# Gating the output weights on GpSimd behind a raw sample mix, and reading the residual from PSUM by halves

## The reference

```python
mod = (c @ w_mod + b_mod)[:, None, :]
sh1, sc1, g1, sh2, sc2, g2 = jnp.split(mod, 6, axis=-1)     # one c for the prompt, another for the sample
...
pool_out, new_pool = _pool_mixer(u, hist_pool, past, w_pool, pool_scale)
attn = _stick_breaking(q, k_all, v_all, q_pos, k_pos).reshape(b, n, SB_WIDTH)
mix = jnp.concatenate([pool_out, attn], axis=-1) @ w_out    # (n, 1024) @ (1024, 1024)
x = _layer_norm(ALPHA * x + (1 + g1) * mix, ln1_g, ln1_b)
hn2 = (_norm(x) * (1 + sc2) + sh2).astype(x.dtype)
```

## Time and profile before

| | |
|---|---|
| median of 3 runs | 804.96 us (803.8 to 807.6) |
| the profiled execution | 804.16 us, its span 802.4 us |
| granted TensorE clock, mean | 0.979 |
| busy in the span | PE 767.7, DVE 562.9, ACT 374.6, POOL 309.9 us |
| block B | from 231 to about 490 us |
| first and last mix (M0 of tile 0, M1 of tile 8) | 299.1 us, 481.0 us |

### The profile page before, as it was taken

How to read it: one execution, slowest core, us unless ns; L and a number is a source line. 1 busy time by engine, 2 the same in 40 slices (tenths; PEclk the granted TensorE clock), 3 DMA queues, 4 the chain that set the end, 5 groups by cost and what they waited for, 6 DMA issues and landing times. The chain is left out here.

```text
span 802.4 us, 13449 instructions
## 1 busy us (share of the span) xinstructions
PE 767.7 (96%) x4808; PEld 606.4 (76%) x4809; DVE 562.9 (70%) x621; ACT 374.6 (47%) x706; POOL 309.9 (39%) x261
## 2 busy tenths in 40 slices
PE   7999999999989899999999997799999999999995
PEld 4889999999975566767767786488888888888641
DVE  5759957762125995876787867998656999574178
ACT  4571212212246983554464528544444444544254
POOL 2100799990010300100000110367565899564156
PEclk9999999999999999999999996899999999999997
DMA  8947644715049701320202249967779998889695
GB/s 320 388 153 257 210 158 133 228 53 185 1 149 327 236 2 53 106 80 27 80 27 79 80 158 333 338 249 262 259 269 361 415 376 270 294 315 364 238 372 200
DMA packets 78442, 168.59 MB, mean 210 GB/s; under 512 B 6974, under 2 KB 32126, under 8 KB 76219
## 3 DMA queue, kind: packets, MB, share of 16 engines
q1 hardware_dynamic: 69154, 134.36, 47.9%
q0 software_dynamic: 8048, 29.36, 9.9%
q10 hardware_dynamic: 1192, 4.21, 1.5%
HBM read 132.57 MB, written 33.12 MB: 207 GB/s over the span
## 5 line engine op out<-in xcount | busy, mean ns | idle before, releaser
L2501 PE MATMUL psum<-we_hi,x_parts 128*128 x384 | 136.5, 402 | 0.8 <-ACT x_parts L2257 0.8
L2045 DVE TENSOR_TENSOR we_lo<-we_raw,we_hi 128x2048 fp32r<-128x2048 f32 x48 | 118.0, 2461 | 1.5
L490 PE MATMUL psum<-hn_hi,w_hi 128*128 128x364 f32 (+1 forms) x380 | 91.2, 332 | 1.3 <-DVE hn_lo L716 1.3
L490 PE MATMUL psum<-hn_lo,w_hi 128*128 128x364 f32 (+1 forms) x380 | 90.3, 329 | 0.0
L490 PE MATMUL psum<-hn_hi,w_lo 128*128 128x364 f32 (+1 forms) x380 | 90.0, 328 | 0.0
L2044 DVE CAST we_hi<-we_raw 128x2048 fp32r<-128x2048 f32 x44 | 59.6, 1355 | 39.5 <-DMA we_raw<-in_w_up_dram 25.6
L1279 PE MATMUL psum<-wo_hi,mixin 128*128 128x512 f32 (+1 forms) x256 | 82.9, 395 | 1.6 <-DVE logits L1646 1.1
L2501 PEld LDWEIGHTS psum<-we_hi,x_parts 128*128 128x128 f32 x384 | 72.1, 188 | 15.3 <-issue 1.1
L2501 PE MATMUL psum<-we_lo,x_parts 128*128 x192 | 75.4, 393 | 0.0
L793 DVE SCALAR_TENSOR_TENSOR proj<-early,cT,proj 128x2048 f32<-128x2048 f32 x28 | 72.1, 2616 | 1.5 <-DMA early<-in_w_mod_dram 1.3
L490 PEld LDWEIGHTS psum<-hn_hi,w_hi 128*128 128x128 f32 x380 | 66.6, 189 | 4.7 <-issue 2.3
(11 more groups left out here) (376 smaller groups left out, 1569.2 us busy)
## 6 DMA issues: line engine op xcount, KB each, us to landing
we_raw<-in_w_up_dram SPq DMA_DIRECT2D x32, 1024.0 KB, 8.4
early<-in_w_mod_dram SPq DMA_DIRECT2D x16, 1024.0 KB, 5.4
we_raw<-in_w_down_dram SPq DMA_DIRECT2D x16, 1024.0 KB, 7.0
w_raw<-in_w_in_dram SPq DMA_DIRECT2D x16, 512.0 KB, 6.2
we_raw<-ff_d SPq DMA_DIRECT2D x12, 512.0 KB, 7.2
proj<-in_x_prompt_dram SPq DMA_DIRECT2D x4, 1024.0 KB, 8.0
sc_room<-in_w_mod_dram SPq DMA_DIRECT2D x4, 1024.0 KB, 11.0
wo_raw<-in_w_out_dram SPq DMA_DIRECT2D x2, 2048.0 KB, 9.4
```

What stands on the lines that cost most here:

```text
L490: mm = pe.matmul(psum[:, 2 * c + slot, 0:n], w[:, slot, k, :], hn[:, k, t0:t0 + n], start=(k == 0 and w is w_hi and hn is hn_hi), stop=(k ...
L2045: dve.tensor_tensor(we_lo[:, a:b], raw, we_hi[:, a:b].bitcast(F32), ALU.subtract).then_inc(ready, 1)
L2501: mm = pe.matmul(psum[:, bank, :], x[:, s, k, :], w[:, bass.ds(at + k * 2 * DE, 2 * DE)], start=(k == 0 and x is x_hi and w is we_hi), sto ...
```

## The change

The sample's mix no longer uses split weights. It becomes the step MS, in four parts at steps 10 to 13: float32 matmuls on `w_out` as loaded, with the two column halves in partitions 0 to 63 and 64 to 127 of bank 7. C0 and C1 of the sample follow at DVE steps 14 and 15, with the sample's gate now in the room of ln1_b. The 48 split matmuls of the sample, its Ph and its Pl are gone.

After the sample's mix GpSimd multiplies the prompt's gate into the eight chunks of `w_out` in place. The splits wh and wl wait for this and move from steps 13 to 22 and 15 to 25 to steps 16 to 23 and 17 to 24. For the prompt's tiles C0, C1 and R become R0 and R1: each reads a half of the mix from PSUM and adds ALPHA times x, with a row sum each; the two sums meet in the operation that makes the mean. The pieces PM are reordered (the sample's four first), GpSimd's constants come before the gates, and the mixes of tiles 1 to 7 move up (M0 of tile 1 from step 31 to 28).

```diff
 DVE_BESIDE = {
-    1: "DV:0", ... 14: "DV:8", 15: "wl:0", 16: "wl:1", 18: "wl:2", ... 25: "wl:7", 26: "Pl:0", 28: "C0:0",
+    1: "DV:0", ... 14: "DV:8 C0:0", 15: "C1:0", 17: "wl:0", 18: "wl:1", ... 24: "wl:7", 26: "Pl:1", 27: "R:0", 28: "E1:0 G1:0 R0:1",
...
+        g1s = l1b
...
+        PIECES = [(g, SEQ, DEC) for g in range(4)] + [(g, t0, 512) for g in range(4) for t0 in (0, 512)]
+        RAW_PARTS = 4
...
-            for dst, src in (mod_row(g1, 1, 2), (l1g, ...), mod_row(sc2, 1, 4), mod_row(sh2, 1, 3)):
+            for dst, src in (mod_row(g1, 0, 2), (l1g, ...), mod_row(sc2, 1, 4), mod_row(sh2, 1, 3)):
                 sp.dma_start(dst, src).then_inc(rows_in, 16)
             sp.wait_ge(pv_done, sample_units)
             sp.dma_start(*x_rows(0)).then_inc(xb_loaded, 16)
-            sp.dma_start(l1b, ln1_b[0].partition_broadcast(P)).then_inc(rows_in, 16)
+            for dst, src in (mod_row(g1s, 1, 2),):
+                sp.dma_start(dst, src).then_inc(g1_in, 16)
...
+            for n in range(KC):
+                k = WO_ORDER[n]
+                pool.wait_ge(rows_in, 16 * 4)
+                pool.wait_ge(mix_done, 2)
+                pool.tensor_tensor(wo_raw[:, k, :], wo_raw[:, k, :], g1, ALU.mult).then_inc(wo_gated, 1)
...
+            def mix_sample(m):
+                if m >= RAW_PARTS // 2:
+                    pe.wait_ge(att_copied, 2 * (m - RAW_PARTS // 2 + 1))
+                if m == 0:
+                    pe.wait_ge(pool_copied, 4)
+                    for half in range(2):
+                        pe.wait_ge(wo_loaded[half], 16)
+                    take("MS", 0, (mix_copied, 2))
+                for k in range(m * KC // RAW_PARTS, (m + 1) * KC // RAW_PARTS):
+                    for half in range(2):
+                        mm = pe.matmul(psum[DEC * half:DEC * half + DEC, 7, :], proj[:, k, SEQ:NT],
+                                       wo_raw[:, k, 512 * half:512 * half + 512], start=(k == 0), stop=(k == KC - 1))
+                if m == RAW_PARTS - 1:
+                    mm.then_inc(mix_done, 2)
...
             def high_wo(n):
-                act.wait_ge(wo_loaded[k // 4], 16)
+                act.wait_ge(wo_gated, n + 1)
...
-            def copy_mix(n, half):
+            def gate_sample(half):
+                dve.wait_ge(mix_done, 2)
+                dve.wait_ge(g1_in, 16)
+                at = slice(DEC * half, DEC * half + DEC)
+                gate = g1s[at, 512 * half:512 * half + 512]
+                dve.tensor_tensor(tile_of(0)[:, 4 * half:4 * half + 4, :], by_chunk(psum[at, 7, :]), by_chunk(gate),
                                   ALU.mult).then_inc(mix_copied, 1)
...
+            def residual(n, half):
+                r, part = rows(ORDER[n]), slice(4 * half, 4 * half + 4)
                 dve.wait_ge(xb_loaded, 16 * (n + 1))
+                dve.wait_ge(mix_done, 2 * n + half + 1)
+                total = (more_sums if half else sums[0])[0:r, n:n + 1]
+                dve.scalar_tensor_tensor(out=tile_of(n)[:, part, :], in0=by_chunk(xb)[0:r, part, :], scalar=ALPHA,
+                                         in1=by_chunk(bank(f"M{half}", n)[0:r, :]), op0=ALU.mult, op1=ALU.add,
+                                         accum_out=total).then_inc(mix_copied, 1)
```

More of the change, by code:

```diff
@@ L1093, in _ @@
                     sp.wait_ge(mix_copied, 2)
-                    for dst, src in (mod_row(g1, 0, 2),):
-                        sp.dma_start(dst, src).then_inc(g1_in, 16)
+                    sp.dma_start(l1b, ln1_b[0].partition_broadcast(P)).then_inc(rows_in, 16)
                 if n == TILES - 1:
@@ L1353, in _ @@
                         pool_map(n)
+                    elif step == "MS":
+                        mix_sample(n)
                     elif step in ("M0", "M1"):
@@ L1456, in square @@
                 if of == 0 and n + 1 < TILES:
-                    act.wait_ge(res_ready, n + 1)
+                    if n == 0:
+                        act.wait_ge(res_ready, 1)
+                    else:
+                        act.wait_ge(mix_copied, 2 * n + 2)
                     act.dma_start(*x_rows(n + 1)).then_inc(xb_loaded, 16)
@@ L1588, in centre @@
                 r = rows(ORDER[n])
-                dve.tensor_scalar(mean[of][0:r, n:n + 1], sums[of][0:r, n:n + 1], -1.0 / D, None, ALU.mult)
-                dve.tensor_scalar(mean32[of][0:r, n:n + 1], sums[of][0:r, n:n + 1], -1.0 / (32 * D), None, ALU.mult).then_inc(summed[of], 1)
-            def residual(n):
-                r, x = rows(ORDER[n]), tile_of(n)
-                dve.wait_ge(xb_loaded, 16 * (n + 1))
-                dve.wait_ge(mix_copied, 2 * n + 2)
-                dve.scalar_tensor_tensor(out=x, in0=by_chunk(xb)[0:r], scalar=ALPHA, in1=x, op0=ALU.mult, op1=ALU.add,
-                                         accum_out=sums[0][0:r, n:n + 1]).then_inc(res_ready, 1)
-                dve.wait_ge(res_ready, n + 1)
-                centre(0, n)
+                for dst, size in ((mean[of], D), (mean32[of], 32 * D)):
+                    if of == 0 and n:
+                        ins = dve.tensor_scalar(dst[0:r, n:n + 1], sums[of][0:r, n:n + 1], more_sums[0:r, n:n + 1], -1.0 / size,
+                                                ALU.add, ALU.mult)
+                    else:
+                        ins = dve.tensor_scalar(dst[0:r, n:n + 1], sums[of][0:r, n:n + 1], -1.0 / size, None, ALU.mult)
@@ new lines, in centre, with residual_sample @@
+                ins.then_inc(summed[of], 1)
+            def residual_sample():
+                r, x = DEC, tile_of(0)
+                dve.wait_ge(xb_loaded, 16)
+                dve.wait_ge(mix_copied, 2)
+                dve.scalar_tensor_tensor(out=x, in0=by_chunk(xb)[0:r], scalar=ALPHA, in1=x, op0=ALU.mult, op1=ALU.add,
+                                         accum_out=sums[0][0:r, 0:1]).then_inc(res_ready, 1)
+                dve.wait_ge(res_ready, 1)
+                centre(0, 0)
+            def residual(n, half):
+                r, part = rows(ORDER[n]), slice(4 * half, 4 * half + 4)
+                dve.wait_ge(xb_loaded, 16 * (n + 1))
+                dve.wait_ge(mix_done, 2 * n + half + 1)
[3 more added lines that the diff above has]
+                                         accum_out=total).then_inc(mix_copied, 1)
+                if half:
+                    dve.wait_ge(mix_copied, 2 * n + 2)
+                    centre(0, n)
@@ L1610, in scale_up @@
                     dst, row = scaled_of(n)[0:r], l1g
+                    if n == 0:
+                        dve.wait_ge(rows_in, 16 * 4)
                 else:
@@ L1663, in _ @@
                     elif step in ("C0", "C1"):
-                        copy_mix(n, int(step[1]))
+                        gate_sample(int(step[1]))
                     elif step == "R":
-                        residual(n)
+                        residual_sample()
+                    elif step in ("R0", "R1"):
+                        residual(n, int(step[1]))
                     elif step in ("E1", "E2"):
```

48 lines of the change are left out of this document (21 added, 27 removed), and 39 rows, old and new, of tables (ACT_BESIDE, DVE_BESIDE, PE_BESIDE).

## The result

| | before | after |
|---|---|---|
| median of 5 runs each, us | 805.84 (803.8 to 807.6) | 826.76 (825.65 to 827.03) |
| ratio of the two | | 1.0256, interval 1.0236 to 1.0276 |
| profiled execution: its time, span | 804.2, 802.4 | 827.0, 825.3 |
| value rows' transfer lands (DVE goes on) | 254.46 | 254.76 |
| first prompt mix starts | 317.08 (step 31) | 320.43 (step 28) |

What follows compares the result with a forecast made beforehand. DVE was taken to bound ahead of the first mix, PE from first to last mix. A 22 us delay less 12.5 saved (11.3 + 1.2) gave +9.5 on 804.2, 813.7, median 814 us; range 801 to 820.

Steps and rivals of the forecast that it cites:

- The delay D: First prompt mix against the sample's first mix at 299.1 us: starts at 321, 22 us later; above 12.5 means slower.
- the parts of MS: On PE ahead of the first mix: column halves overlap, about 1.9 us per part, four parts 7.5 us.
- the wait for bank 7: On PE in step 16: the first PM piece waits for C1 to free the bank, between 277 and 286 us.
- the end of the gates: On GpSimd: eight products of 2.37 us from about 267.5 us, stretched by turns with DVE, the last ending near 291.
- The gates in turns: Ahead of the first mix: GpSimd's gates and two-input DVE instructions exclude each other, adding 17.6 us; forecast case, chance 0.55.
- The scans are in: DVE's scans, with two SBUF inputs, also take turns with GpSimd's gates; held about three to one.
- a DVE list that ends at 302: DVE's list ahead of the first mix without gates: 267.4 plus 34.8 us of work, before adding 17.6.
- Nothing else of this size hides there: From first to last mix: PE is full, idle only 1.6 us, so all 11.3 us of sample mix come off.
- the mix doesn't lose what it should: Rival in the mixes: DVE or ACT become the bound there; dropped for DVE's 50 us to spare, no chance given.
- D of 9.5: Rival with gates in DVE's gaps, chance 0.17: PE alone decides, first mix at 308.5, 9.5 us later, net -3 us.
- The tail: Behind the last mix: one half residual of 0.8 us replaces product and residual, so 1.2 us comes off.

Runs made afterwards that it cites:

- 5: Kernel after without gates in the output weights, gate products from PSUM and full residuals as before, order lists of before from step 26 on: 807.54 us, ratio 0.9997 to before.
- 4: Kernel after with the order lists of the kernel before from step 26 on, all else as after: 819.48 us, ratio 1.0151 to before.
- 6: Kernel after without the eight gate products and with the order lists of before from step 26 on: 809.06 us, ratio 1.0014 to before.
- 1: Kernel after with the eight gate products on GpSimd left out: 816.57 us, ratio 1.0136 to before.
- kernel 7: Kernel after with each gate product on GpSimd replaced by memsets of about the same length: 817.74 us, ratio 1.0103 to before.
- 8: Kernel after with tile 5's second-norm square on ScalarE and the small DVE operation following it one step later: 821.22 us, ratio 1.0163 to before.
- 9: Raw sample mix alone in the order lists of before, its four parts at steps 8, 9, 10 and 12: 809.52 us, ratio 1.0022 to before.
- 11: Raw sample mix alone, parts early, lists of before; both sample gate products at DVE step 14, first PM piece behind them at step 17: 805.98 us, ratio 0.9988 to before.

## Why the prediction was wrong in size

The difference in E parts as follows, each step from a pair of kernels: the raw sample mix ahead of the mixes instead of M0 and M1 in them +2.4 us (5 against before), the gates' turns +9.4 (4 against 6), the re-timed lists +6.9 (after against 4): 18.7, measured 18.6. The steps form a chain from before to after, so they must add up; the check is that the other way round gives nearly the same, 8.8 us for the gates (after against 1) and 7.4 for the lists (1 against 6). Up to 2 us of the first step are the slow first part of kernels 5 and 6, and belong to the gates instead. With 0.3 us of later landing and a tail 4.0 us longer that is the span's 22.9, where the sum had 9.5: of the missing 13.4 us 8.2 stand ahead of the last mix's end, which came 18.9 us later where 22 less 11.3 had been forecast, and 5.2 behind it.

- **The delay D, right in number, in part by luck.** 21.3 us against 22. Within it the parts of MS (1.9 us forecast, 1.94 measured), the wait for bank 7 (283.4, forecast between 277 and 286) and the end of the gates (290.7, forecast 291) came as said; without gates D is 10.9 (kernel 1, corrected for the landing), forecast 9.5.
- **The gates in turns, right in kind.** The scans are in, which I had at three to one. Their size was too large: I counted 17.6 us exposed. DVE's busy time up to the first low part rose by 14.3 us (22.5 against 8.2 in kernel 7, which takes 269.62 to 281.34 with 3.25 and 0.46 us idle); kernel 7's idle 3.3 us lay under them, and 11.0 us came through to the first low part, 10.2 to the first mix. That the sum was right nonetheless is luck, two errors that cancel: I added 17.6 to a DVE list that ends at 302, which isn't where the first mix stands without gates: there PE's own list and its wait for bank 7 put it near 309.
- **"Nothing else of this size hides there": the step that failed.** I let all 11.3 us of the sample's mix come off behind the first mix. 2.4 came off. The prediction has PE full there, so that each microsecond of matmul taken out comes off the end. The rival "the mix doesn't lose what it should" was in the text and I dropped it, because DVE had 50 us to spare: an argument from a sum of busy time, against waits that are decided one at a time. The waits come from the lists, in which the prompt tiles' mixes and norms stand two to five steps earlier, beside other units' scans and copies (the square of tile 5 in step 48 instead of 53). There it stands in front of ACT's attention copy while DVE is not yet done with what it needs. With the lists of before PE idles for 1.5 us and 6.9 of the lost 8.9 us are back (experiments 4, 5, 6), with one square moved 3.2 of them (8). I had looked at these lists for what they do ahead of the first mix only.
- **The 11.3 us against MS's cost, too kind even so.** In the lists of before the exchange costs 2.4 us (5) where D of 9.5 less 11.3 had promised a gain of 1.8. Bank 7 and the clock that PE loses around it are most of it: with the parts early the cost is 1.9 (9), and with the bank freed a step earlier and asked for a step later the exchange gives 1.5 us of E (11).
- **The tail, wrong.** Of the 1.2 us promised behind the last mix 0.4 came: a logits addition now stands ready between the half residual and the scale-up and waits 0.44 us for PE, and the next step waits 0.33 for the square. The tail as a whole is 4.0 us longer: the stretch to the first experts 51.0 us against 48.6, the last stretch 48.3 against 46.7, with 226.0 us of experts equal between them. These are the stretches whose clock is not full (0.77 and 0.85, before 0.79 and 0.89):

```profile
499.99:551.00 51.01, 39.96 (x319) 30.47 (x319) 40.60 (x98) 30.80 (x49) 14.18 (x14) 0.77 0.82 293
551.00:777.00 226.00, 225.80 (x1117) 182.72 (x1116) 161.92 (x91) 107.03 (x203) 140.74 (x90) 1.00 0.86 312
777.00:825.30 48.30, 39.03 (x88) 15.64 (x86) 34.80 (x38) 20.27 (x34) 23.20 (x25) 0.85 0.72 272
```

PE's busy time for the same instructions is 39.96 and 39.03 us here, 38.45 and 36.94 before. Of the tail's 4.0 us, 3.6 are thus in PE's busy time at the lower clock. Whether the change causes that is open: the profiles of kernels with the same code there have tails of 322.1 us (8) to 325.5 (4), so the one profile of the kernel before, with 321.3, may lie low.

## What to carry to other kernels

Price a removed piece of work by the waits of the list that stands behind it, not by the sum of busy time: a full engine loses what is taken out only if everything it waits for keeps its lead, and lists that are re-timed for a shorter stage want the same reading, wait by wait, as the stage they were written for. Work moved to GpSimd that reads SBUF beside DVE instructions with two SBUF inputs isn't free: here it cost more than the same work on DVE (11.2 us against 7.1), and memsets of the same length cost nothing that can be told. Change the order and the algorithm in separate steps: here the order alone held 7 of 20 us, and one square in front of a copy held 3.

## What I hadn't expected of the hardware

- TENSOR_TENSOR_SCAN with ring and mask in SBUF alternates with GpSimd's products one instruction at a time: a pair of 256 columns takes 4.92 us instead of 1.27; beside memsets it takes 1.27.
- A wait of some 3 us on PE is paid twice: behind 3.35 us idle the scores took 2.08 us instead of 1.13, behind 2.47 us idle a part of MS took 3.68 instead of 1.94. The granted clock shows the lower level (1.2 GHz) just where the slow instructions stand: 0.52 from 438.8 to 442.2 us, 0.50 from 256.2 to 259.8 in kernel 5.
- A power on GpSimd, one element in each partition, is on record with 2.58 us beside a scale-up and a scan on DVE, and with 0.54 at 438.70, where no such instruction ran. It held nothing up here: it was over before DVE's list came to the instruction that needs it.
